# A two-block transformer forward pass on one core: projection work reordered around the decay masks, and the residual added inside the expert accumulators

## The chip, the cores and the metric

The kernel runs on one core of a Trainium2 chip. The metric is device time in microseconds (us), from start to end of one execution. Every weight and the input come from HBM, and the 256 x 1024 result goes back to it.

TensorE (PE) multiplies matrices into PSUM, eight banks of 128 x 512 fp32. VectorE (DVE) and ScalarE (ACT) move data out of PSUM and do elementwise work, GpSimd (POOL) does a little, and SyncE (SP) issues nearly all DMAs. Each engine runs its own program in order and waits on semaphores that the others raise.

## The reference, cut to what matters

There are 256 tokens of width 1024. The first block has a token mixer (a spatial gating branch and a gated delta rule branch) and a mixture of 32 experts. The second block has two attention layers, each with a gated feed-forward network.

```python
# first block
qkv = silu(causal_dwconv(dn_qkv, dn_conv_w))          # 4 taps along the tokens
q, k, v = split(qkv)                                  # 8 heads of 128 each
q = q * rsqrt(sum(q * q) + 1e-6); k = k * rsqrt(sum(k * k) + 1e-6)
G = cumsum(g)                                         # in chunks of 64 tokens
decay = exp(where(causal, G_i - G_j, -inf))
lmat = where(strict, beta * (k @ k.T) * decay, 0)     # solved as (I + lmat)^-1
attn = (q @ k.T) * decay
h = layer_norm(ALPHA * h + mix)                       # ALPHA = 2 ** 0.25
ffn = hier_moe(h)                                     # two of 32 experts a token
h = layer_norm(ALPHA * h + ffn)                       # the end of the first block
# second block
h = h + even_mixer(rmsnorm(h), ...)                   # begins with a projection of width 448
```

## The kernel before

**Weights.** The weights stream through a ring of SBUF slots, 2 MB each, filled by SP in the fixed order of `stream_items`. The mixer uses four slots and the experts six. SP refills a slot when its last reader has signalled.

**A projection tile.** Products are made of three fp32r matmuls each: high x high, high x low, low x high. So each half of a slot (a pair in the code) must be split first: ACT copies it rounded into a high part (`split_high`, `next_high`, L1067 to L1085), then DVE subtracts that from the slot and leaves the low part (`split_low`, L1565). `split_pairs` numbers the pairs. PE waits in `split_chunk` (L407) for the low part, then `project_split` issues 48 matmuls of 128 x 256 into one bank. There are two buffers for the high parts, so the high part of pair n waits until PE has finished pair n - 2.

**Order in the mixer.** The four tiles of `w_pa` (pairs 13 to 16) come before four key tiles (`dn_k`, 17 to 20), four query tiles (`dn_q`, 21 to 24) and four value tiles (`dn_v`, 25 to 28). After the second value pair of tiles come the column sums of the squared keys (`square_sums`, L570), then the last two value tiles, key-key products in `chunk_pairs`, the query sums, the first half of `dn_z`, the key transposes, the query-key products, and the second half of `dn_z`. All of these take their bank from a rotation of four (`take` without a bank); a fixed bank is given otherwise. A bank that is taken again waits until its reader has emptied it.

**Decays.** Four groups of matmuls (`Gb`) and two more (`Gc`) give sums of the log decays. DVE clips them, ACT takes the exponentials (L1151 to L1158), and DVE multiplies them by masks of 64 x 64 blocks (L1662 to L1674). DVE then clears the first four columns of six staging buffers (`stage_zero`, L1678).

**Convolution.** For each tile ACT copies two 128 x 256 halves out of PSUM into staging buffers, adding the bias (L1187), multiplies each by the last of the four taps (L1195), and splits the next pair (`next_high`, L1196). DVE splits the low part and adds the three other taps (L1700). ACT then applies SiLU two tiles late, squares the result, and for the keys and the queries `inverse_norm` turns the column sums into factors by Ln and Exp; DVE multiplies by them (`normed`, L1680).

**Experts and the seam.** The expert loop (`Fori` over 16 pairs of experts) adds each expert's output into four PSUM banks (`acc0` to `acc3`) by one-hot matmuls (`scatter`). The banks are opened by a product of the identity with a column of zeros (L722). After the loop DVE raises `experts_done` (L2006), ACT and DVE split the two pairs of the first weight of the second block (`lora`, pairs 45 and 46), and `residual` (L1807) computes h * ALPHA + acc for four pieces of 128 x 512, each followed by its statistics; `layer_norm` (L1528) subtracts the mean, waits for the factor and scales. The root-mean-square norm of the second block follows, then PE transposes and projects.

What sets the order everywhere is the program of each engine as written; no planner is at work.

## Time and profile before

| | |
|---|---|
| median of three runs | 1641.43 us (1639.04 to 1644.94) |
| the profiled execution's own time | 1639.78 us |
| its span, first to last instruction | 1638.0 us |
| PE busy with matmuls | 1433.2 us (87%) |
| DVE busy | 681.5 us (42%) |
| ACT busy | 542.7 us (33%) |
| DMA engines in the 20 slices of the experts | nearly always nine tenths or more |
| mean granted TensorE clock | 0.934 of full speed |

The busy shares are averages over stages with different limits. In the experts' stage the transfers are busy all the time; in the mixer and in the second block PE is busy nearly all the time, except for stretches in which it waits for ACT or DVE. "Idle before" in a row is the time in which the engine did nothing ahead of that row, with what ended it. In the rows that join several instructions, the first number is the start, the second the time from the first start to the last end.

### The profile page before, as it was taken

To read this page: it belongs to the slowest core of one execution; us is meant where nothing else is said; L and a number is where in the kernel's file an instruction comes from. 1 tells how busy PE (TensorE), PEld (TensorE's weight loads), DVE (VectorE), ACT (ScalarE), POOL (GpSimd) and SP (SyncE) were. 2 spreads that over 40 slices of the span, in tenths; PEclk is the share of its full clock that TensorE was granted. 3 is DMA by queue.
4 is the path that set the end of the run, shared out by engine and by line. 5 is a ranking of instruction groups with operands and counts; after the bars stand their busy time and mean duration, and the time that the engine had idled before them with its cause. 6 is when DMAs were issued, how large, how long until landed. Compare 5 with 4: busy or idle time off the path is not lost.

```text
span 1638.0 us, 25680 instructions
## 1 busy us (share of the span) xinstructions
PE 1433.2 (87%) x10764; PEld 1152.2 (70%) x10764; DVE 681.5 (42%) x1030; ACT 542.7 (33%) x861; POOL 46.8 (3%) x53
## 2 busy tenths in 40 slices
PE   6999887999968888888888849958999987889997
PEld 6989887987855444444444429547999986689997
DVE  4435676535640110101101144574555546555554
ACT  2451686135320110100101024344433345553343
POOL 0000000400020000000000000000000000000000
PEclk8988999989979999999999979978999998999999
DMA  6531442211266999999999982202544532154420
GB/s 285 192 118 52 154 155 80 77 53 59 83 280 274 427 427 429 429 429 427 429 429 429 428 372 102 105 1 92 204 177 183 218 112 94 52 193 181 178 102 26
DMA packets 27434, 349.54 MB, mean 213 GB/s; under 512 B 3041, under 2 KB 3297, under 8 KB 4578
## 3 DMA queue, kind: packets, MB, share of 16 engines
q1 hardware_dynamic: 27218, 347.46, 52.9%
q8 instruction: 54, 0.88, 0.2%
q10 hardware_dynamic: 144, 1.05, 0.2%
q14 instruction: 18, 0.15, 0.0%
HBM read 347.45 MB, written 1.05 MB: 213 GB/s over the span
## 4 chain that ended last, share of the span: by engine, by line
PE 68%; DMA 14%; DVE 9%; ACT 5%; issue 2%; SPq 1%; PEldq 0%; POOL 0%; DVEq 0%; POOLq 0%; ACTq 0%
PE psum L405 67%; DMA ring<-in_w 14%; ACT pages L1050 2%; DVE slot_lo L1573 2%; ACT mix_hi L1079 1%; PE psum L474 1%; DVE pages L2036 1%; DVE pages L2068 1%; DVE pages L2040 0%; DMA ab<-in_w_ab 0%; ACT pages L1305 0%; DVE pages L1538 0%; PE psum L758 0%; PEldq L815 0%; DVE pages L1700 0%
## 5 line engine op out<-in xcount | busy, mean ns | idle before, releaser
L405 PE MATMUL psum<-ring,pages 128*64 128x256 f32 (+1 forms) x2564 | 361.2, 439 | 66.5 <-DMA ring<-in_w 47.8
L405 PEld LDWEIGHTS psum<-ring,pages 128*64 128x64 f32 x2564 | 186.9, 143 | 225.9 <-issue 81.9
L405 PE MATMUL psum<-x_hi,gu_hi 128*128 128x256 f32 x704 | 201.3, 286 | 3.8 <-DVE x_lo L1560 3.8
L405 PE MATMUL psum<-x_lo,gu_hi 128*128 128x256 f32 x704 | 201.2, 286 | 0.0
L405 PE MATMUL psum<-x_hi,gu_lo 128*128 128x256 f32 x704 | 201.1, 286 | 0.0
L405 PE MATMUL psum<-h_hi,mix_hi 128*128 128x256 f32 x512 | 151.8, 296 | 17.2 <-DVE slot_lo L1573 8.9
L405 PE MATMUL psum<-pages 64*64 64x64 f32 (+10 forms) x1752 | 135.6, 267 | 21.5 <-ACT pages L1050 10.8
L1573 DVE TENSOR_TENSOR slot_lo<-ring,mix_hi 128x2048 fp32r<-128x2048 f32 x44 | 102.3, 2329 | 120.0 <-ACT mix_hi L1079 119.8
L405 PE MATMUL psum<-h_lo,mix_hi 128*128 128x256 f32 x512 | 149.7, 292 | 0.0
L405 PE MATMUL psum<-h_hi,slot_lo 128*128 128x256 f32 x512 | 149.5, 292 | 0.0
L405 PEld LDWEIGHTS psum<-pages 64*64 64x64 f32 (+4 forms) x1752 | 109.8, 156 | 45.5 <-issue 20.2
L405 PEld LDWEIGHTS psum<-x_hi,gu_hi 128*128 128x128 f32 x704 | 137.1, 195 | 6.1 <-DVE x_lo L1560 2.4
L405 PEld LDWEIGHTS psum<-x_lo,gu_hi 128*128 128x128 f32 x704 | 137.1, 195 | 1.6
L405 PEld LDWEIGHTS psum<-x_hi,gu_lo 128*128 128x128 f32 x704 | 137.0, 195 | 0.0
L1976 DVE TENSOR_TENSOR pages<-pages,psum 128x256 f32<-128x256 f32 x32 | 13.5, 421 | 268.2 <-ACT pages L1302 268.2
L405 PEld LDWEIGHTS psum<-h_hi,mix_hi 128*128 128x128 f32 x512 | 103.6, 202 | 19.6 <-DVE slot_lo L1573 13.8
L2084 DVE TENSOR_TENSOR gu_lo<-ring,gu_hi 128x2048 fp32r<-128x2048 f32 x44 | 100.8, 2292 | 27.2 <-ACT gu_hi L1384 27.2
L474 PE MATMUL psum<-consts,pages 128*128 128x128 f32 x262 | 46.0, 338 | 73.9 <-DVE pages L2132 31.2
L405 PEld LDWEIGHTS psum<-h_lo,mix_hi 128*128 128x128 f32 x512 | 103.6, 202 | 0.1
L405 PEld LDWEIGHTS psum<-h_hi,slot_lo 128*128 128x128 f32 x512 | 103.2, 202 | 0.0
L1302 ACT ACTIVATE pages<-psum 128x256 f32<-128x256 f32 x32 | 12.3, 385 | 274.2 <-PE psum L405 274.2
L1079 ACT ACTIVATE mix_hi<-ring 128x2048 fp32r<-128x2048 f32 x44 | 84.0, 1908 | 44.2 <-PE psum L405 44.2
(220 smaller groups left out, 2120.4 us busy)
## 6 DMA issues: line engine op xcount, KB each, us to landing
ring<-in_w SPq DMA_DIRECT2D x96, 2048.0 KB, 18.0
ring<-in_ffn SPq DMA_DIRECT2D x44, 1536.0 KB, 6.5
ring<-in_w_in SPq DMA_DIRECT2D x16, 2048.0 KB, 8.1
ring<-in_e_in SPq DMA_DIRECT2D x3, 2048.0 KB, 15.8
ring<-in_w_pa SPq DMA_DIRECT2D x2, 2048.0 KB, 8.0
ring<-in_w_pb SPq DMA_DIRECT2D x2, 2048.0 KB, 8.7
ring<-in_w_o SPq DMA_DIRECT2D x2, 2048.0 KB, 8.1
ring<-in_e_out SPq DMA_DIRECT2D x2, 2048.0 KB, 15.0
```

The lines of the kernel that those rows point to most:

```text
L405: return pe.matmul(o, lhsT, rhs, start=start, stop=stop, skip_group_check=True)
L474: last = pe.transpose(o[:, j * P:(j + 1) * P], s, ident)
L1050: st.do(act_e.activation(o, i, func, **kw), name)
L1079: act_e.activation(high[:, 0:size], slot(n)[:, c * size:(c + 1) * size], ACT.Copy).then_inc(S("w_high"), 1)
L1302: act_e.activation(silu[:, r, :], psum[:, r, 0:T], ACT.Silu).then_inc(S("silu_ready"), 1)
L1573: ve.tensor_tensor(slot_low[slot_no(n)][:, sl], slot(n)[:, sl], high[:, 0:size], ALU.subtract).then_inc(S("w_split"), 1)
L1976: ve.tensor_tensor(acts[:, r, :], silu[:, r, :], psum[:, r, T:2 * T], ALU.mult).then_inc(free[r], 1)
L2036: do(ve.scalar_tensor_tensor(e[:, h2, :], bias, slope(g), v[:, 0:SPAN], ALU.mult, ALU.add), f"{sec}s{g}")
L2068: do(ve.tensor_tensor(e[:, :, sl], e[:, :, sl], z[:, :, b].unsqueeze(2).broadcast_to([P, 2, size]), ALU.mult), f"{sec}_probs" if b else None)
L2084: ve.tensor_tensor(gu_part["lo"][j % 2], slot(item_no[(nm, 0)] + j)[:, 0:gu_size], gu_part["hi"][j % 2], ALU.subtract).then_inc(S("gu_spli ...
```

## The change

In the mixer: ACT computes the decay exponentials before it splits the `w_pa` and the first key pairs, not after them. The six staging buffers are cleared earlier, behind the splitting of the `w_pa` input. DVE's multiplications by the masks move to the first value tile. ACT splits the next pair ahead of the last tap instead of behind it. For the value tiles DVE, not ACT, multiplies by the last tap. The square sums get banks 4 to 7, and the key-key products take rotating banks. DVE multiplies the keys by their factors ahead of the split of that place, not behind it.

At the seam: the accumulator banks are opened by ALPHA times the identity, multiplied with the normed tokens, so that they hold h * ALPHA + ffn when the experts are done. DVE takes the statistics and the first step of the norm straight from PSUM. The last pair of experts is written out behind the loop on ACT and DVE, and the two `lora` pairs are split inside it, into buffers of their own (pages 5 and 7). SP issues the first three weights of the second block before it reads the largest expert's count, not after.

```diff
...
         split_pairs = []
-        page_high = {n: part(f"w_hi{n}", n * PAGE, PAGE) for n in (1, 2, 3, 4, 5)}
+        page_high = {n: part(f"w_hi{n}", n * PAGE, PAGE) for n in (1, 2, 3, 4, 5, 7)}
         page_part = {n: part(f"in{n}", n * PAGE, PAGE).rearrange("p (k t) -> p k t", t=T) for n in (1, 2, 3, 4, 6, 8, 9)}
...
                     name = f"{part}_ss{q4}"
-                    o = take(name)
+                    o = take(name, 4 + q4)
                     for half in range(2):
...
             for g in range(2):
-                chunk_pairs(f"kk{g}", 4 + g, lambda j, r: (units(3)[:, unit(g, j), r], units(3)[:, unit(g, j), r]))
+                chunk_pairs(f"kk{g}", None, lambda j, r: (units(3)[:, unit(g, j), r], units(3)[:, unit(g, j), r]))
             square_sums("q", 7)
...
                 o = take(f"acc{n}", 4 + n)
-                mm(o, ident, col("zero").broadcast_to([P, HALF]), True, False)
+                mm(o, alpha_ident, piece(tm(0), n), True, False)
             pe.wait_ge(*V("onehot_ready", NB))
...
             highs = (page_high[2], page_high[3])
-            project_tokens("lora", [("e_in", 0)], highs, parts, spread_done("att0"), LORA)
+            project_tokens("lora", [("e_in", 0)], (page_high[5], page_high[7]), parts, spread_done("att0"), LORA)
             project_split("qB", [("e_in", 1)], highs, parts)
...
             input_high(page_part[8], fm(5), lambda i: V("ya_ready", i + 1))
-            split_high(18)
 
...
             act(mix, mix, ACT.Exp, "decay_ready", scale=-1.0)
+            split_high(18)
 
...
 
-            stage = lambda n: page(5)[:, n % 6 * 260:n % 6 * 260 + 260]
             act_e.wait_ge(*V("stage_zero", 6))
...
                     act_e.sem_inc(free[place[name][0]], 1)
-                    for half in range(2):
+                    next_high()
+                    for half in range(2 if part != "dn_v" else 0):
                         k = 2 * n + half
                         act(fm(pg)[:, k, :], stage(8 * s + k)[:, 4:260], ACT.Copy, "tapped", scale=col("conv", 3 * 24 + first + k))
-                    next_high()
                     for b2 in (at - 3, at - 2):
...
                     act_e.activation(actT[:, r, :], psum[:, 2 + r, 0:T], ACT.Copy).then_inc(free[2 + r], 1)
+                if last and phases >= 3:
+                    split_high(MIXER_PAIRS + 2)
                 for r in range(2):
...
                     y_high(r, slot_table[:, 0, bass.ds(it * 2 + (EXPERTS + r), 1)]).then_inc(S("y_high"), 1)
+
+            with act_e.Fori(0, EXPERTS // 2 - 1) as it:
+                expert_pair(it)
+            expert_pair(EXPERTS // 2 - 1, True)
             tables_at[0] = None
...
                 act_e.dma_start(page(10), io["c_attn"]).then_inc(S("attn_tables"), 16)
-            if phases >= 3:
-                split_high(MIXER_PAIRS + 2)
             layer_rstd(2)
...
                     h, b = piece(tm(0), n), n % NB
-                    do(ve.scalar_tensor_tensor(h, h, mean_var[:, b, 0:1], piece(gains, n // NB * NB), ALU.subtract, ALU.mult))
+                    src = bank_of(f"{banks}{n}") if banks else h
+                    do(ve.scalar_tensor_tensor(h, src, mean_var[:, b, 0:1], piece(gains, n // NB * NB), ALU.subtract, ALU.mult),
+                       f"{banks}{n}" if banks else None)
                 ve.wait_ge(*V("norm_rstd", no + 1))
...
                     h, b = piece(tm(0), n), n % NB
-                    ve.wait_ge(st.sem, start + n + 1)
+                    if banks:
+                        ve.wait_ge(*evacuated(f"{banks}{n}"))
+                    else:
+                        ve.wait_ge(st.sem, start + n + 1)
                     do(ve.scalar_tensor_tensor(h, h, rstd[:, b:b + 1], piece(gains, n // NB * NB + 1), ALU.mult, ALU.add),
...
             input_low(0, page_part[9], fm(5), page_part[8])
+            ve.wait_ge(S("h_split"), 4)
+            for n in range(6):
+                do(ve.memset(stage(n)[:, 0:4], 0.0), "stage_zero")
 
...
 
+            cd = ab[:, 128:160]
+
+            def masked_decays():
+
+                ve.wait_ge(*V("decay_ready", 1))
+                do(ve.tensor_tensor(mix, mix, chunk_mask("minus_first", UNITS), ALU.mult))
+                do(ve.tensor_tensor(mix_t, mix_t, decay, ALU.mult))
+                do(ve.tensor_tensor(decay, decay, chunk_mask("incl_up", UNITS), ALU.mult))
+                settle()
+                for b in range(NB):
+                    m = mix.rearrange("p (h b) t -> p h b t", b=NB)[:, :, b, :]
+                    do(ve.tensor_tensor(m, m, bc(ab[:, 16 + b * HEADS:16 + (b + 1) * HEADS], 2, [P, HEADS, CHUNK]), ALU.mult))
+                for q4 in range(4):
+                    ve.wait_ge(*evacuated(f"Gb{q4}"))
+                do(ve.tensor_copy(cd, exp_rows.rearrange("p (x t) -> p x t", t=CHUNK)[:, :, CHUNK - 1]))
+                settle()
+
             for at in range(24):
                 s, k = at // 8, at % 8
-                if at % 2 == 0:
-                    split_low(19 + at // 2)
+                if at == 16:
+                    masked_decays()
                 if at == 20:
...
                     normed("k", 3, 8)
+                if at % 2 == 0:
+                    split_low(19 + at // 2)
                 dst = fm(CONVS[s][1])[:, k, :]
                 src = stage(at)
-                ve.wait_ge(*V("tapped", at + 1))
+                if s < 2:
+                    ve.wait_ge(*V("tapped", at + 1))
+                else:
+                    ve.wait_ge(*V("staged", at + 1))
+                    do(ve.tensor_scalar(dst, src[:, 4:260], col("conv", 3 * 24 + CONVS[s][2] + k), None, ALU.mult))
                 for j in range(3):
-                    if j:
+                    if j or s == 2:
                         settle()
...
                                 ALU.add), "router")
+            do(ve.tensor_scalar(alpha_ident, ident, ALPHA, None, ALU.mult))
             ge = r11[:, 80:96].rearrange("p (b g) -> p b g", b=NB)
...
                     spread_slots(r, slot_table[:, 0, bass.ds(it * 2 + r, 1)])
+                if last and phases >= 3:
+                    split_low(MIXER_PAIRS + 1)
                 for r in range(2):
...
                     y_low(r, slot_table[:, 0, bass.ds(it * 2 + (EXPERTS + r), 1)]).then_inc(free[2 + r], 1)
+                if last and phases >= 3:
+                    split_low(MIXER_PAIRS + 2)
+
+            with ve.Fori(0, EXPERTS // 2 - 1) as it:
+                expert_pair(it)
+            expert_pair(EXPERTS // 2 - 1, True)
             st.last = (free[3], base[3] + EXPERTS)
...
                         y_low(0, slot_table[:, c, bass.ds(e + EXPERTS, 1)]).then_inc(S("more_split"), 1)
-                ve.wait_ge(*V("more_split", EXPERTS * (MAX_PASSES - 1) + BUILT))
+                ve.wait_ge(*V("more_scattered", EXPERTS * (MAX_PASSES - 1)))
             do(ve.memset(ab[:, 0:1], 0.0), "experts_done")
-            if phases >= 3:
-                split_low(MIXER_PAIRS + 2)
-            residual(ALPHA, [f"acc{n}" for n in range(4)], layer_stats)
+            ve.wait_ge(*V("scattered", EXPERTS + 2))
+            for n in range(4):
+                layer_stats(n, bank_of(f"acc{n}"))
             ve.wait_ge(*V("ln2_landed", 16))
-            layer_norm("ln2", 2, tm(1))
+            layer_norm("ln2", 2, tm(1), "acc")
             if phases < 3:
...
                         sp.dma_start(slot(n + 2), src).then_inc(landed[slot_no(n + 2)], 16)
+                early = moe_first + 3 * EXPERTS
+                if phases >= 3:
+                    for n in range(early, early + MORE):
+                        load(n, *items[n])
                 sp.wait_ge(*V("starts_ready", 1))
...
                 with sp.If(most > CAP):
-                    for n in range(moe_first + 3 * EXPERTS - SLOTS, moe_first + 3 * EXPERTS):
+                    for n in range(early - SLOTS + MORE, early):
                         sp.wait_ge(*released[n])
...
```

ACT's program from the splitting of the `w_pa` input (L1092 here, L1097 in the changed kernel) to the first key tile. `mix_hi` rows are high parts, `ab` and `pages` rows at 128x32 and 128x1024 are exponentials. Before:

```order
L1092 ACTIVATE in_86<-pages 128x512 x4
L1079 ACTIVATE mix_hi<-ring 128x2048 x4
L1041 ACT_TABLE_LOAD
L1050 ACTIVATE pages<-psum 128x512 x4
L1050 ACTIVATE ab<-ab 128x32
L1050 ACTIVATE pages<-pages 128x1024 x2
L1050 ACTIVATE pages<-psum,consts 128x256 x2
L1050 ACTIVATE pages<-pages,consts 128x256 x2
L1079 ACTIVATE mix_hi<-ring 128x2048
```

The same place in the changed kernel:

```order
L1097 ACTIVATE in_87<-pages 128x512 x4
L1046 ACT_TABLE_LOAD
L1055 ACTIVATE pages<-psum 128x512 x4
L1055 ACTIVATE ab<-ab 128x32
L1055 ACTIVATE pages<-pages 128x1024 x2
L1084 ACTIVATE mix_hi<-ring 128x2048 x4
L1055 ACTIVATE pages<-psum,consts 128x256 x2
L1084 ACTIVATE mix_hi<-ring 128x2048
L1055 ACTIVATE pages<-pages,consts 128x256 x2
```

The seven exponentials and their table load now stand before four high parts, and the next high part stands before the taps.

DVE's program of the changed kernel at the seventh and eighth query and the first value tile. Before, the five rows at the masks stood ahead of the first key tile's split, and no TENSOR_SCALAR stood among the value tiles:

```order
L1587 TENSOR_TENSOR slot_lo_61<-ring,mix_hi 128x2048
L1722 SCALAR_TENSOR_TENSOR pages<-pages,consts 128x256 x6
L1691 TENSOR_TENSOR pages<-pages,masks 128x1024
L1692 TENSOR_TENSOR pages<-pages 128x1024
L1693 TENSOR_TENSOR pages<-pages,masks 128x1024
L1697 TENSOR_TENSOR pages<-pages,ab 128x8x64 x2
L1700 COPY ab<-pages 128x32
L1587 TENSOR_TENSOR slot_lo_62<-ring,mix_hi 128x2048
L1718 TENSOR_SCALAR pages<-pages,consts 128x256
L1722 SCALAR_TENSOR_TENSOR pages<-pages,consts 128x256 x3
```

The masks stand between the last tile of the queries and the split for the third value tile.

DVE's program of the changed kernel in the last pair of experts, written out behind the loop:

```order
L2000 TENSOR_TENSOR pages<-pages,psum 128x256 x2
L1988 TENSOR_SCALAR spots<-pages 128x256 x2
L1587 TENSOR_TENSOR slot_lo_61<-ring,w_hi_80 128x1792
L1992 SCALAR_TENSOR_TENSOR y_lo<-psum,pages,y_hi 128x512 x2
L1587 TENSOR_TENSOR slot_lo_61<-ring,w_hi_81 128x1792
```

Before, the two rows of 128x1792 stood behind `experts_done` and ahead of four pairs of SCALAR_TENSOR_TENSOR and BN_STATS; those pairs are now four BN_STATS that read PSUM.

## Rows read from the trace of the kernel before

**Rows 1.** Stretch, length, busy of PE PEld DVE ACT POOL, clock, DMA share, GB/s

```profile
183.00:188.00 5.00, 4.45 (x21) 4.45 (x22) 4.86 (x8) 3.73 (x4) 0.00 (x0) 0.50 0.03 7
```

**Rows 2.** Waits of PE from 130 to 360: us in total, times, longest

```profile
PE psum L405 <- ACT pages L1050: 9.7, 3, 4.8
PE psum L405 <- DVE slot_lo L1573: 8.2, 4, 7.2
```

**Rows 3.** Chain of waits, 130 to 310: start, us, what

```profile
172.30 1.23 DVE pages L1663
...
183.56 8.11 PE psum L405 x48
...
221.95 11.78 PE psum L405 x96
...
240.69 8.47 PE psum L405 x48
...
255.11 2.49 DVE pages L1685 x4
...
268.14 8.42 PE psum L405 x48
...
285.30 13.80 PE psum L405 x160
```

**Rows 4.** PE in order of time, 227 to 241: start, us, instructions

```profile
233.55 3.62 PE L405 MATMUL psum<-pages,consts 128*128 128x256 f32 x16
```

**Rows 5.** ACT in order of time, 120 to 300

```profile
177.51 0.84 ACT L1050 ACTIVATE pages<-psum,consts 128x256 f32<-128x256 f32 x2 [5.31 <-DVE pages L1678]
178.47 0.91 ACT L1050 ACTIVATE pages<-pages,consts 128x256 f32<-128x256 f32 x2
179.28 1.89 ACT L1079 ACTIVATE mix_hi<-ring 128x2048 fp32r<-128x2048 f32 x1
...
238.57 1.28 ACT L1041 ACT_TABLE_LOAD   x1
239.86 2.42 ACT L1050 ACTIVATE pages<-psum,consts 128x512 f32<-128x512 f32 x4
242.16 2.20 ACT L1050 ACTIVATE pages<-pages 128x512 f32<-128x512 f32 x4
```

**Rows 6.** DVE in order of time, 120 to 300

```profile
181.21 2.29 DVE L1573 TENSOR_TENSOR slot_lo<-ring,mix_hi 128x2048 fp32r<-128x2048 f32 x1 [3.79 <-ACT mix_hi L1079]
183.42 2.96 DVE L1700 SCALAR_TENSOR_TENSOR pages<-pages,consts 128x256 f32<-128x256 f32 x6
```

**Rows 7.** DVE in order of time at the seam, 930 to 990

```profile
961.84 0.06 DVE L2006 MEMSET ab<- 128x1 f32 x1 [1.20 <-issue]
964.16 3.96 DVE L1573 TENSOR_TENSOR slot_lo<-ring,w_hi 128x1792 fp32r<-128x1792 f32 x2 [2.26 <-ACT w_hi L1079]
968.14 0.69 DVE L1817 SCALAR_TENSOR_TENSOR pages<-pages,psum 128x512 f32<-128x512 f32 x1
...
973.60 0.28 DVE L1532 BATCH_NORM_AGGREGATE tiny<-tiny 128x2 f32<-128x12 f32 x2
...
976.71 2.73 DVE L1543 SCALAR_TENSOR_TENSOR pages<-pages,tiny 128x512 f32<-128x512 f32 x4
```

**Rows 8.** ACT in order of time at the seam, 930 to 990

```profile
954.74 0.38 ACT L1305 ACTIVATE pages<-psum 128x256 f32<-128x256 f32 x1 [4.11 <-PE psum L758]
...
959.05 0.69 ACT L1294 ACTIVATE y_hi<-psum,pages 128x512 fp32r<-128x512 f32 x1 [3.35 <-PE psum L405]
...
962.43 3.28 ACT L1079 ACTIVATE w_hi<-ring 128x1792 fp32r<-128x1792 f32 x2 [2.69 <-DVE ab L2006]
```

**Rows 9.** PE in order of time at the seam, 950 to 984

```profile
982.14 2.18 PE L474 MATMUL psum<-consts,pages 128*128 128x128 f32 x9 [20.24 <-DVE pages L2132]
```

**Rows 10.** SP's issues, 925 to 962, in order of time

```profile
932.72 0.35 SPq L2299 DMA_DIRECT2D ring<-in_e_lora  x1
```

**Rows 11.** DMA issues by line, 925 to 962: KB each, median us to landing

```profile
ring<-in_e_lora SPq DMA_DIRECT2D x1, 1792.0 KB, 20.3
```

48 lines of the change are left out of this document (18 added, 30 removed).

## The prediction, made before the changed kernel had run

> **What bounds the kernel now.** The slices of the page come first. In the slices of the experts the transfers are busy at nine tenths or more, so that stage moves as a whole with whatever comes ahead of it and cannot be shortened by this change. In the mixer and in the second block PE is busy nearly all the time, so there only its waits and its clock can be won. The waits of PE in the mixer come next: 8.2 us for low parts from DVE, of which one wait is 7.2 us, and 9.7 us for results of ACT in three waits, the longest 4.8 us [rows 2]. The chain of waits then shows what each wait is. The long one ends at 183.56, when the third key tile starts. Ahead of it stand DVE's mask products from 172.30, ACT's staging of the first key tile at 177.51, which had been idle 5.31 us for DVE, a high part at 179.28 and a low part at 181.21 [rows 3, 5, 6]. PE pays twice for such a wait. After it the granted clock is 0.50 of full speed, the 1.2 GHz level [rows 1], and the tile at 183.56 takes 8.11 us; two tiles at full clock take 233.55 - 221.95 = 11.60 us, 5.80 each [rows 3, 4]. So a tile after a wait costs 2.3 us more; those at 240.69 and 268.14 cost 2.7 and 2.6 more [rows 3].
>
> At the seam PE stands idle for 20.24 us until 982.14 [rows 9]. That is one serial chain on DVE and ACT: `experts_done` at 961.84, ACT's two high parts from 962.43, DVE's two low parts from 964.16, the residual with its statistics from 968.14 to 973.60, the first step of the norm, and the first finished tokens from 976.71 [rows 7, 8].
>
> **The mixer, step by step.** I count in the clock of the profiled execution. The exponentials wait for the clipped decays, and ACT's next task ahead of the change is a high part that waits for PE; ACT idles there, so the exponentials cost nothing at their new place. With the staging buffers cleared long before, ACT stages the first key tile as soon as PE has it, and the third key tile starts 7.2 us earlier, at 176.3, with no wait.
>
> Can PE then go on without waits? Behind a full tile ACT needs 0.96 us to stage it (177.51 to 178.47) and 1.9 us for the high part (179.28 to 181.21), now without the taps between them, and DVE 2.2 us for the low part (181.21 to 183.42) [rows 5, 6]. That is 5.1 us of the 5.80 of a tile, which leaves 0.7 us. DVE's own work for a tile is 2.2 + 2.9 = 5.1 us, also below 5.80. So the three smaller waits of 1.0 us in all [rows 2] go as well. Eight tiles from 176.3 end at 176.3 + 8 x 5.80 = 222.7, where the key sums start; before it was 233.55 [rows 4]. Gain here 10.8 us.
>
> The key sums take 3.6 us [rows 4] and end at 226.3. Before, the next tile then waited for a bank that ACT's Ln had to empty (one of the three ACT waits). With the sums in banks 4 to 7 it waits only for its low part. DVE ends the taps of the eighth tile at 211.1 (tile full) + 0.96 + 1.9 + 2.2 + 2.9 = 219.1. The masks now stand here: 172.30 to 177.4, 5.1 us [rows 3, 5], to 224.2, and the low part to 226.4. The eleventh tile starts at 226.5, against 240.69 [rows 3]: gain 14.2. So the masks are hidden just to the end; had they been 2 us longer, PE would lose those 2 us.
>
> A value tile costs DVE two more multiplications of 128 x 256. The trace has none of this form here. The nearest rows are DVE's taps, 2.96 us for six [rows 6], 0.49 each; nothing is the lower bound. I take 0.4 each, since they read one tensor, so 3.7 us of taps a tile (2.9 to 3.9). DVE ends the ninth tile's taps at 230.1, the low part at 232.3. The twelfth tile runs from 232.4 to 238.2. ACT turns 230.1 into the key factors: SiLU and square 0.9 (estimated from the tap pair, 0.91 for two, and the four Exp, 2.20), table load 1.28, four Ln 2.3, four Exp 2.2 [rows 5], 236.8. DVE's tenth tile ends at 236.0 and the key products of `normed`, 2.4 us [rows 3], end at 238.4. The key-key products start at 238.5; before, `normed` ended at 255.11 + 2.49 = 257.6. Gain 19.1.
>
> The query side: ACT stages and splits the eleventh tile (2.8), loads SiLU (1.3), does SiLU and square (1.3), 242.2, then stages and splits the twelfth, 245.0. DVE's low part waits for 239.6 and ends at 241.8, its taps at 245.5, and the last square comes at 246.4. The first `dn_z` tile starts behind the last query sum at about 247.3, against 268.14 [rows 3]: gain 20.8. From there ACT and DVE are late, not PE. DVE: low part 247.7, taps 251.4. ACT: SiLU 0.4, table 1.28, Ln 2.3, Exp 2.2, table 1.28, staging of `dn_z` 0.9 and high part 1.9, 261.6. DVE: low part 263.9, query `normed` 2.4, 266.3. The query-key products start at 266.4, against 285.30 [rows 3]: gain 18.9. PE is idle some 3 us ahead of the last query sum and again ahead of 266.4, so two spells at the low clock are likely. The first falls on `dn_z`, where PE has time to spare. The second falls on the 13.80 us of [rows 3] that ran undisturbed before; I take 2.4 us for it (the three prices above are 2.3, 2.7 and 2.6), or nothing if PE's transposes keep the clock up. **Mixer: 18.9 - 2.4 = 16.5 us** (14 to 20). Behind that, up to the experts, the order is unchanged, and the experts' transfers start as much earlier.
>
> **The seam.** In the last pair ACT's copy ends at 954.74 + 0.38 = 955.1. The two high parts, 3.28 us, now run there, to 958.4; the last `y_hi` has to wait for PE until 959.05 in any case, and the one ahead of it takes 0.7, so it is on time to 0.1 us [rows 8]. They need the weight `e_lora` landed: 932.72 + 20.3 = 953.0, 2.1 us before 955.1 [rows 10, 11]. DVE's first low part (1.98, half of 3.96) runs beside them. The second stands behind the last `y_lo` and ahead of `experts_done`, which therefore moves from 961.84 to 963.8. Behind `experts_done`, before: 961.84 to 973.60, 11.8 us. Now: four statistics at 0.69 us each, 2.7 us, at 966.5. The norm from there is the same in number and size, 3.1 us to the first tokens (973.60 to 976.71), 969.7 [rows 7]. **Seam: 976.7 - 969.7 = 7.0 us**. The bounds: statistics from PSUM at 0.5 to 1.0 us each give 6 to 8, and the low clock after the wait can end a tile earlier or later, 1 us each way.
>
> The trace shows DVE with operands from both memories at this size: the residual reads PSUM and takes 0.69 us, the last step of the norm reads SBUF and takes 2.73 / 4 = 0.68 [rows 7]. The Trainium skill, "VectorE: DVE Perf Modes", in the section on the TRN2 errata, gives VectorE 120 cycles of fixed cost from PSUM against 58 from SBUF, an estimate of 0.065 us more for each of the eight instructions that now read PSUM. By that rule the seam would give 6.5 us and the forecast would be 0.5 us later; by the rows it gives 7.0. The rows decide.
>
> The rest: ALPHA times the identity is one small DVE instruction in the router's chain, 0.2 us. Opening the banks is the same four matmuls with other data, nothing. The early clears (six of 0.1 us) stand beside PE's decay sums, nothing. The SP loads moved ahead of the count were issued at once before too, nothing.
>
> **Sum.** 16.5 + 7.0 - 0.2 = 23.3 us. The profiled execution took 1639.78 us (span 1638.0 and 1.8 around it), so 1616.5; it lies 1.65 us below the median of 1641.43, and the median of the changed kernel should be **1618 us**.
>
> **The rivals.** (a) Only the front of the mixer holds. If DVE or ACT run late among the value tiles (the cover of the masks is 0.1 us, and ACT's switches of tables stand in the new chain), PE gets the 10.8 us of the front and gives back what follows: 10.8 + 7.0 - 0.2 = 17.6, 1623.8. For it: four table loads lie on the new path. Against: the sums above were made with them, and the last wait has 0.7 us of slack a tile until then.
>
> The trace has a table load of 1.28 us, and the next instruction starts 0.01 us behind it [rows 5]. The Trainium skill, "ScalarE: Activation LUTs", section "What ACT_TABLE_LOAD costs", gives 2.66 us for every switch, a drain of 1.38 among them. By that rule the four loads would make the path 5.5 us longer and the time 1623.5. The row shows no drain, so its chance is 0.02.
>
> (b) The seam gives nothing: the high parts wait for `e_lora`, because more transfers are in flight with it, and the last `y_hi` is late by 7 us. 23.3 - 7.0 = 16.3, 1625.1. Against: it landed 2.1 us before it is needed.
>
> (c) The other side, slower: the same wait, but long. ACT stands at `e_lora` with `y_hi` behind it, and PE's scatter, `experts_done` and all of the second block behind that. Each microsecond that it lands after 955.1 costs one. It is slower than before from 955.1 + 23.3 = 978 on; at 990 the time is 1618 + 35 = 1653. For it: the queue is full there. Against: all transfers of that stretch are done soon after 962.
>
> (d) The change doesn't do what it says: a wait that I didn't see keeps the first key tile's staging where it was and the chain at the seam as long, 1641.
>
> (e) More than forecast: no spell at the low clock ahead of the query-key products and luck with the clock at the seam, 2.4 + 2 and a lower price of the taps, 1: 1612.
>
> **How the numbers follow.** Forecast, 1613 to 1624: 0.66. (a) 0.14, the rule on table switches 0.02, (b) 0.07, (e) reaching below 1613: 0.05, (d) 0.03, (c) 0.03. Within 0.3%, 4.9 us, is about what a measurement of this kernel can't tell from no change. So faster 0.66 + 0.14 + 0.02 + 0.07 + 0.05 = 0.94, same 0.03, slower 0.03. The range takes in (e), (a) and (b) with a little above them for the bounds: 1611 to 1628.
>
> **What would show it.** Right: PE's wait ahead of the third key tile gone and that tile at 5.8 us; key sums starting at about 223, `dn_z` at about 247, query-key products at about 266; at the seam `experts_done` some 2 us later against the last copy of ACT, and PE's idle time at 13 us, not 20.24. Wrong: a wait of PE for a low part behind the masks, a wait of ACT for the landing of `e_lora`, statistics from PSUM well above 0.69 us, or a part of the mixer gain given back between 300 and 490.

## The result, and the profile after

The changed kernel takes 1615.88 us (median of 4 runs, 1612.46 to 1618.32) against 1640.24 us of the kernel before in the same comparison (4 runs, 1638.95 to 1644.94). The ratio is 0.9845, 95% interval 0.9816 to 0.9873. The forecast was 1618, with a range of 1611 to 1628. The span of the profiled execution fell from 1638.0 to 1615.2 us, by 22.8.

Waits of PE in the same part of the mixer (131.2 to 344): us in total, times, longest. They are to be compared with [rows 2].

```profile
PE psum L410 <- ACT pages L1055: 4.7, 2, 3.3
PE psum L410 <- DVE pages L1684: 3.3, 1, 3.3
...
PE psum L410 <- DVE slot_lo L1587: 0.4, 1, 0.4
```

The 8.2 us for low parts have become 0.4, and the 9.7 us for ACT 4.7. The wait of 3.3 us for DVE's query product (L1684), ahead of the query-key products, has grown: it was 1.24 us before. The chain that ended last, from 165 on, is to be compared with [rows 3]:

```profile
164.99 47.05 PE psum L410 x392
...
220.20 1.13 DVE pages L1691
...
225.07 2.29 DVE slot_lo L1587
...
265.27 2.50 DVE pages L1684 x4
267.81 15.33 PE psum L410 x160
```

The first row is what the forecast said of the front of the mixer: PE multiplies 47 us on end (the row begins where the view does), straight through the place of the wait of 7.2 us. Behind it the chain runs over DVE: the masks (L1691 and on), low parts, taps. The last row is the one that took 13.80 us in [rows 3].

The places at which PE still waits, in order of time (start, us, instructions, idle time before them and what ended it):

```profile
247.61 2.07 PE L410 MATMUL psum<-pages,consts 128*128 128x256 f32 x4 [3.26 <-ACT pages L1055]
...
267.81 0.91 PE L410 MATMUL psum<-pages 128*64 128x64 f32 x12 [3.35 <-DVE pages L1684]
```

And the granted clock (the figure behind the busy times of the five engines) in the stretch of [rows 1], and behind these two waits:

```profile
183.00:188.00 5.00, 5.00 (x44) 5.00 (x44) 4.26 (x7) 4.44 (x8) 0.00 (x0) 1.00 0.24 102
```

```profile
247.30:250.70 3.40, 3.09 (x10) 2.73 (x11) 3.29 (x6) 0.31 (x2) 0.00 (x0) 0.51 0.00 0
267.80:271.20 3.40, 3.38 (x64) 3.39 (x64) 2.76 (x2) 0.00 (x0) 0.00 (x0) 0.50 0.11 48
```

The stretch that ran at the 1.2 GHz level before runs at full speed. In this execution two spells of 3.4 us at the 1.2 GHz level are left, where the forecast put them.

**How stretches are compared.** Two profiled executions don't line up. The first tile of `w_pa` starts at 141.51 before and at 142.66 after, though the change touches nothing that PE waits for ahead of it; in the twelve experiments below this start lies between 139.67 and 144.91. So from here on every time in the mixer is counted from the first `w_pa` tile, and every time at the seam from ACT's last copy. The value transposes are the end of the mixer's changed part:

| counted from the first `w_pa` tile | before | after | gain |
|---|---|---|---|
| third key tile starts | 42.05 | 34.65 | 7.40 |
| key sums start | 92.04 | 80.73 | 11.31 |
| eleventh tile starts | 99.18 | 84.76 | 14.42 |
| first `dn_z` tile starts | 126.63 | 106.46 | 20.17 |
| query-key products start | 143.79 | 125.15 | 18.64 |
| value transposes start | 157.42 | 140.32 | 17.10 |

Four traces below hold the changed mixer instruction by instruction: this one, `mixer_only`, `splits_back` and `ident_moved`. Up to the query-key products they agree within 0.02 us (125.14 to 125.16). Behind them they don't: the value transposes start at 140.32, 141.27, 141.22 and 141.32. The last three are alike, and the trace above is the odd one, by 1 us. So a difference at the query-key products counts from a few tenths on, one at the value transposes only above 1 us, and the mixer's gain is 16.1 to 17.1.

**The seam.** DVE in order of time, to be compared with [rows 7]:

```profile
942.40 2.02 DVE L1587 TENSOR_TENSOR slot_lo<-ring,w_hi 128x1792 fp32r<-128x1792 f32 x1 [6.51 <-ACT w_hi L1084]
944.57 1.44 DVE L1992 SCALAR_TENSOR_TENSOR y_lo<-psum,pages,y_hi 128x512 fp32r<-128x512 f32 x2
945.93 2.02 DVE L1587 TENSOR_TENSOR slot_lo<-ring,w_hi 128x1792 fp32r<-128x1792 f32 x1
947.87 0.69 DVE L1535 BATCH_NORM_STATS2 tiny<-psum 128x6 f32<-128x512 f32 x1
947.89 0.06 DVE L2038 MEMSET ab<- 128x1 f32 x1
948.48 1.87 DVE L1535 BATCH_NORM_STATS2 tiny<-psum 128x6 f32<-128x512 f32 x3
950.46 0.28 DVE L1541 BATCH_NORM_AGGREGATE tiny<-tiny 128x2 f32<-128x12 f32 x2
950.88 2.72 DVE L1548 SCALAR_TENSOR_TENSOR pages<-psum,tiny,pages 128x512 f32<-128x512 f32 x4
953.52 2.73 DVE L1557 SCALAR_TENSOR_TENSOR pages<-pages,tiny 128x512 f32<-128x512 f32 x4
```

ACT, to be compared with [rows 8]:

```profile
940.40 0.38 ACT L1310 ACTIVATE pages<-psum 128x256 f32<-128x256 f32 x1 [4.11 <-PE psum L763]
940.68 3.28 ACT L1084 ACTIVATE w_hi<-ring 128x1792 fp32r<-128x1792 f32 x2
943.86 1.36 ACT L1298 ACTIVATE y_hi<-psum,pages 128x512 fp32r<-128x512 f32 x2
```

PE's restart and the weight's landing, for [rows 9] and [rows 11]:

```profile
958.95 1.33 PE L479 MATMUL psum<-consts,pages 128*128 128x128 f32 x5 [11.47 <-DVE pages L2164]
```

```profile
ring<-in_e_lora SPq DMA_DIRECT2D x1, 1792.0 KB, 20.1
```

From ACT's last copy to the first tokens it was 976.71 - 954.74 = 21.97 us and is 953.52 - 940.40 = 13.12: the seam gives 8.85 us. The other ten traces with the whole new seam have 13.12 or 13.13 as well. PE's idle time fell from 20.24 to 11.47. The order of L1535 and the memset of L2038 shows a detail that the forecast missed: `experts_done` comes when the second low part has just ended, with no idle time ahead of it.

**The balance.** Gains: 17.10 + 8.85 = 25.95. Losses: 1.15 ahead of `w_pa` (phase, see above), 1.07 in the router (below), 0.54 over the experts and 0.39 behind the seam, 3.15 in all. 25.95 - 3.15 = 22.80, the difference of the spans. This is one pair of executions. The medians of the same comparison differ by 24.4 us.

### The profile page after: what moved, and what is told of

Same layout as the page of the kernel before. It is cut to its first block, busy times and chain, and to the rows that moved or that the text cites. A ratio compares the mean times of both kernels' runs of the same rounds, so it can differ in the third digit from the quotient of the medians.

```text
span 1615.2 us, 25662 instructions
## 1 busy us (share of the span) xinstructions
PE 1432.0 (89%) x10764; PEld 1149.9 (71%) x10764; DVE 682.2 (42%) x1035; ACT 540.5 (33%) x853; POOL 46.8 (3%) x53
## 3 DMA queue, kind: packets, MB, share of 16 engines
q10 hardware_dynamic: 144, 1.05, 0.2%
HBM read 347.45 MB, written 1.05 MB: 216 GB/s over the span
## 4 chain that ended last, share of the span: by engine, by line
PE 69%; DMA 15%; DVE 9%; ACT 4%; issue 2%; SPq 1%; POOL 0%; DVEq 0%; POOLq 0%; ACTq 0%
PE psum L410 67%; DMA ring<-in_w 14%; ACT pages L1055 2%; DVE slot_lo L1587 2%; PE psum L479 1%; DVE pages L2068 1%; DVE pages L1722 1%; ACT mix_hi L1084 1%; DVE pages L2100 1%; DVE pages L2072 0%; DMA ab<-in_w_ab 0%; DVE pages L1548 0%; PE psum L763 0%; ACT pages L1310 0%; DVE pages L2155 0%
## 5 line engine op out<-in xcount | busy, mean ns | idle before, releaser
L410 PE MATMUL psum<-pages 64*64 64x64 f32 (+10 forms) x1760 | 145.6, 275 | 20.4 <-ACT pages L1055 10.2
L410 PEld LDWEIGHTS psum<-pages 64*64 64x64 f32 (+4 forms) x1760 | 115.3, 161 | 48.4 <-issue 24.1
L479 PE MATMUL psum<-consts,pages 128*128 128x128 f32 x262 | 48.1, 348 | 65.1 <-DVE pages L2164 22.8
L1055 ACT ACTIVATE pages<-psum 128x512 f32<-128x512 f32 (+4 forms) x82 | 48.0, 600 | 153.2 <-PE psum L410 126.9
```

What stands on the lines that cost most here:

```text
L410: return pe.matmul(o, lhsT, rhs, start=start, stop=stop, skip_group_check=True)
L479: last = pe.transpose(o[:, j * P:(j + 1) * P], s, ident)
L1055: st.do(act_e.activation(o, i, func, **kw), name)
```

## The experiments

Twelve kernels, each executed 4 to 8 times beside the kernel before. A ratio is always to that. Single executions of one kernel spread over 3 to 12 us here, so a difference of 3 us between two kernels is read from the stretches of the trace, and the times only bear it out.

### The two parts of the change alone

`seam_only` has the mixer of the kernel before, instruction by instruction, and the changed seam. `mixer_only` is the reverse; its core:

```diff
-                mm(o, alpha_ident, piece(tm(0), n), True, False)
+                mm(o, ident, col("zero").broadcast_to([P, HALF]), True, False)
...
-                if last and phases >= 3:
-                    split_high(MIXER_PAIRS + 2)
...
-            for n in range(4):
-                layer_stats(n, bank_of(f"acc{n}"))
+            if phases >= 3:
+                split_low(MIXER_PAIRS + 2)
+            residual(ALPHA, [f"acc{n}" for n in range(4)], layer_stats)
```

> The kernel before with only the seam of the change (high and low parts in the last pair, ALPHA times the identity in the accumulators, statistics and norm from the banks, SP's loads moved). Every instruction of the mixer stands as it was. Theory of the forecast (the two parts act apart, seam 7.0 less 0.2): 1640.2 - 6.8 = 1633.4. Reading of the two traces: from ACT's last copy to the first tokens 21.97 us before and 13.12 after, 8.85, less 1.06 us that PE stands longer ahead of the rank product: 7.8, 1632.4. Rival (the seam's gain is luck with the clock behind the wait, which goes when the stretch moves in time): 5 to 6, 1634.5 to 1635.

> The changed kernel with the seam as before and without ALPHA times the identity. Theory of the forecast: 1640.2 - 16.5 = 1623.7. Reading of the two traces: the value transposes start 17.1 us earlier against the first tile of w_pa, 0.5 us of it is given back up to the experts: 1623.6. If the two parts act apart, this gain and that of the seam alone add up to the 24.8 us of the whole. Rival (they share something, such as a granted clock that falls elsewhere): the two gains differ from the whole by over 2 us.

Measured: `seam_only` 1632.23 us, ratio 0.9954 (0.9933 to 0.9974), which is 7.5 us by the ratio and 6.5 by the medians (1638.73 before). `mixer_only` 1618.46 us, ratio 0.9894 (0.9874 to 0.9915), 17.4 us by the ratio and 20.3 by the medians. Together the two give 24.9 us by the ratios, the whole change 25.4 (0.0155 x 1640), and 26.8 against 24.4 by the medians. The intervals are about 3.4 us wide to each side, so the times alone don't settle whether the parts add up to within 2 us. The traces do: in `seam_only` copy to tokens is 13.13 us and the mixer is 157.40 long, as before; in `mixer_only` the mixer has the changed kernel's times and copy to tokens is 21.58. So the two parts act apart, as the sum of the forecast supposed, and the seam's gain isn't luck with the clock.

### The front of the mixer: three edits that need each other

`exps_back` puts the exponentials behind the 18th high part again, `masks_back` the masks ahead of the first key pair's low part, `exps_masks_back` both.

```diff
 # exps_back, ACT
+            split_high(18)
             for q4 in range(4):
                 v = await_full(act_e, f"Gb{q4}")
...
-            split_high(18)
 # masks_back, DVE
-                if at == 16:
+                if at == 0:
                     masked_decays()
```

> The changed kernel with ACT's exponentials behind the 18th high part again, where they stood before; nothing else. In the changed trace ACT stages the first key tile at 171.81. With the exponentials (table 1.28, then 4.3 us) from 168.0 on it is free at 173.6, 1.8 us late, and the third key tile starts 1.8 us late, plus 2.3 us for the low clock behind the wait: +4.1, of which the wait of 0.41 us ahead of the eleventh tile hides some, 1619.5. Rival (the exponentials cost only through the mask products that wait for them, and these now stand later): no difference, 1615.9.

> The changed kernel with the mask products ahead of the first key tile's low part again (the staging buffers are still cleared early and the exponentials early). They would run from 170.9 to 176.0 on DVE, where the low part of the third key tile starts at 174.84 in the changed trace: 1.2 us late, so PE waits 1.1 us ahead of the third tile, plus 2.3 us for the low clock: +3.4 there. DVE has 5.1 us more among the value tiles, where PE waited 0.41 us: -0.4. So 1618.9. Rival (masks are the whole cause of the long wait of 7.2 us before): +7 or more, 1623. Rival (DVE's slack absorbs it): 1615.5.

> The changed kernel with both the exponentials behind the 18th high part and the mask products ahead of the first key tile's low part, as before; the staging buffers are still cleared early. Counted from the start of w_pa's first tile, the third key tile starts at 42.05 in the kernel before, 34.65 in the changed one, 35.93 with the exponentials alone moved back and 35.58 with the masks alone. Theory (the two add up in a chain: exponentials to 30.9, masks 5.1 to 36.0, low part 2.3 to 38.3): 38.3, and the clearing of the buffers, which let ACT stage only behind the masks, had cost the other 3.8 us. Rival (exponentials and masks are the whole of the wait): 42. Rival (they don't add up): 36 to 37. Time: the changed kernel's +0 to +2, since the masks at this place give back about 3.5 us at the query sums.

Measured: `exps_back` 1613.94 us, ratio 0.9855 (0.9832 to 0.9878). `masks_back` 1611.10, 0.9829 (0.9807 to 0.9850). `exps_masks_back` 1616.32, 0.9861 (0.9838 to 0.9884). From the first `w_pa` tile:

| | third key tile | wait ahead of it | key sums | `dn_z` | value transposes |
|---|---|---|---|---|---|
| before | 42.05 | 7.2 | 92.04 | 126.63 | 157.42 |
| after | 34.65 | none | 80.73 | 106.46 | 140.32 |
| `exps_back` | 35.93 | 1.14 | 82.11 | 107.39 | 141.66 |
| `masks_back` | 35.58 | 0.76 | 81.75 | 102.47 | 136.78 |
| `exps_masks_back` | 38.10 | 3.29 | 85.75 | 106.47 | 141.70 |

The third key tile comes near the place where the theory had it: 1.28 us later for 1.8 expected, 0.93 for 1.1 or 1.2, and 38.10 for 38.3 with both. Two expected times missed, 1619.5 for `exps_back` and 1618.9 for `masks_back`, since each held 2.3 us for a spell at the low clock that didn't come. The exponentials alone cost 1.3 us, the masks alone 0.9, both together 3.45. In the times this doesn't show: `exps_back` can't be told from the changed kernel. The last 3.95 us up to 42.05 are in `exps_masks_back` no longer there. In the trace before, DVE idles 3.79 us between the clearing of the staging buffers and that low part [rows 6], while ACT, which had waited for the clearing, stages the tile and makes the high part [rows 5]; here the low part follows the masks at once. That points at the late clearing, though no kernel put it back by itself (the order of ACT's work on a pair changed on that stretch too). So the wait of 7.2 us was one chain of three links. That each edit alone would have left most of it is likely from this, but not shown: no kernel made one edit alone.

The other half of the result was in none of the expectations: with the masks back at the front the mixer is *shorter* than in the changed kernel, by 3.54 us at the value transposes and by 3.27 at the query-key products (121.88 for 125.15). DVE in `masks_back`, at the third key tile:

```profile
173.18 1.23 DVE L1691 TENSOR_TENSOR pages<-pages,masks 128x1024 f32<-128x1024 f32 x1
...
178.14 2.29 DVE L1587 TENSOR_TENSOR slot_lo<-ring,mix_hi 128x2048 fp32r<-128x2048 f32 x1
```

5.1 us of masks make PE wait 0.76 us there. In the changed kernel the same 5.1 us stand ahead of the eleventh tile (220.20 in the chain above), on the path that ends last: the query sums wait 3.26 us for it. `masks_back` has no wait at the query sums at all. My expectation priced only the wait of 0.41 us ahead of the eleventh tile and named the wrong sign for the whole. The time agrees in sign (1611.10 for 1615.88), but the two intervals overlap.

### The banks of the square sums, and the taps

```diff
 # squares_back, PE
-                    o = take(name, 4 + q4)
+                    o = take(name)
...
-                chunk_pairs(f"kk{g}", None, ...
+                chunk_pairs(f"kk{g}", 4 + g, ...
 # taps_back, ACT and DVE
-                    for half in range(2 if part != "dn_v" else 0):
+                    for half in range(2):
...
-                    do(ve.tensor_scalar(dst, src[:, 4:260], col("conv", ...), None, ALU.mult))
```

> The changed kernel with the banks of the key and query square sums taken in turn again (and the key-key products in banks 4 and 5), where the eleventh tile needs a bank that ACT's Ln empties. In the changed trace the key sums end at 227.01, the first SiLU behind them starts at 229.22 and the first Ln at 233.30. Theory (the bank was one of the waits won): the eleventh tile starts at 233.9 or so, not 227.42, +6.5 there; PE's later waits of 3.26 and 3.35 us belong to ACT and DVE and take a part of it: the value transposes +4 to +6.5 against the first tile of w_pa, time of the changed kernel +4 to +6.5. Rival (the query chain on DVE is the end anyway, the bank costs nothing): 0 to +1.

> The changed kernel with the first tap of the value tiles on ACT again (0.89 us for two there) and not on DVE (0.76 us for two, pitch 0.38). Theory (DVE ends last at the query sums, since the mask products stand among its value tiles): DVE ends 4 x 0.76 = 3.0 us earlier over the four value tiles, ACT later by 3.6 but with idle time: the wait of 3.26 us ahead of the last query sum shrinks, the time goes down by 1 to 3. Theory of the forecast (ACT's chain with its table loads is the end there, the tap's move takes 0.9 a tile off it): +1 to +3.6.

Measured: `squares_back` 1625.67 us, ratio 0.9924 (0.9899 to 0.9949); value transposes at 147.65, 7.3 us later than in the changed kernel, query-key products 8.9 later. Expected were 4 to 6.5. The medians differ by 9.8 us. PE in its trace, the eleventh tile, and ACT's load of the Ln table and the Ln that it waited for:

```profile
234.18 0.55 PE L410 MATMUL psum<-h_hi,mix_hi 128*128 128x256 f32 x1 [7.12 <-ACT pages L1055]
```

```profile
232.05 1.28 ACT L1046 ACT_TABLE_LOAD   x1
233.34 2.42 ACT L1055 ACTIVATE pages<-psum,consts 128x512 f32<-128x512 f32 x4
```

PE starts when the first Ln has read its bank. So the bank theory holds, and these two lines of the change are worth more than any other edit that was taken back: 7.3 us.

`taps_back` 1615.48 us, ratio 0.9861 (0.9838 to 0.9883): its time can't be told from the changed kernel's. In the trace the query-key products start at 123.91, 1.24 us *earlier* than in the four traces with the changed mixer. So moving the tap to DVE costs 1.2 us in this change. The cost doesn't arise at the query sums, where my theory had it: the last of them starts 0.38 us *later* in `taps_back`, behind a wait of 3.61 us and not 3.26. It arises behind them. ACT's last SiLU of a value tile waits for DVE's taps and starts at 108.58 instead of 109.82, again 1.24 us, and the table load, the Ln of the query norm and the query-key products follow it. The multiplication itself costs 0.38 us (L1718 0.35, the next instruction 0.38 behind its start), against the 0.4 that the forecast took.

### The parts of the seam

```diff
 # splits_back
-                if last and phases >= 3:
-                    split_high(MIXER_PAIRS + 2)
...
             do(ve.memset(ab[:, 0:1], 0.0), "experts_done")
+            if phases >= 3:
+                split_low(MIXER_PAIRS + 2)
```

> The changed kernel with the first two high and low parts of the second block behind experts_done again; the residual stays in the accumulators. Theory: experts_done 0.4 us earlier against ACT's last copy (7.1), then 6.3 us for the parts ahead of the statistics as in the kernel before (961.84 to 968.14): first tokens 5.9 us later, 19.0 us behind the copy and not 13.12; time of the changed kernel +5.9. The other part of the seam, the residual in the accumulators, is then worth 21.97 - 19.0 = 3.0. Rival (the forecast's own terms: the last low part delays experts_done by 2.0): the parts are worth 4.2 only, +4.2.

Measured: 1617.07 us, ratio 0.9872 (0.9851 to 0.9893). DVE behind the last pair (ACT's copy is at 936.50):

```profile
943.31 0.06 DVE L2033 MEMSET ab<- 128x1 f32 x1 [1.20 <-issue]
945.62 3.96 DVE L1586 TENSOR_TENSOR slot_lo<-ring,w_hi 128x1792 fp32r<-128x1792 f32 x2 [2.25 <-ACT w_hi L1084]
949.50 2.48 DVE L1534 BATCH_NORM_STATS2 tiny<-psum 128x6 f32<-128x512 f32 x4
...
955.16 1.40 DVE L1556 SCALAR_TENSOR_TENSOR pages<-pages,tiny 128x512 f32<-128x512 f32 x2
```

First tokens 18.66 us behind the copy (19.0 expected), PE idle for 17.22. So the early splits are worth 18.66 - 13.12 = 5.5 us and the residual in the accumulators 21.97 - 18.66 = 3.3 (2.9 against `mixer_only`, where `experts_done` comes as early as here). The time differs from the changed kernel's by 1.2 us in the medians and 4.4 by the ratios, less than 5.5. In this trace PE did the router product mostly at full clock and reached the rank product 3.8 us earlier against the value transposes (169.92 and not 173.74), which hides most of it in a single execution. The idle time of 1.20 marked "issue" ahead of the memset is the count's load and the branch. With the low part queued ahead of it this time runs beside the low part, and that is what the forecast's +2.0 for `experts_done` left out.

### ALPHA times the identity, and a lock between DVE and GpSimd

PE's gap ahead of the rank product was 5.18 us before. After:

```profile
456.72 0.85 PE L410 MATMUL psum<-pages,consts 128*128 128x32 f32 x3 [6.24 <-DVE pages L1911]
```

DVE and GpSimd (POOL) in the trace after:

```profile
450.67 1.14 DVE L1856 TENSOR_SCALAR pages<-consts 128x128 f32<-128x128 f32 x1
```

```profile
449.93 1.81 POOL L2264 MEMSET pages<- 128x2048 f32 x1
```

```diff
 # ident_moved: from behind the router's bias to behind the picks
-            do(ve.tensor_scalar(alpha_ident, ident, ALPHA, None, ALU.mult))
...
             do(ve.tensor_tensor(pick, r11[:, 320:384], r11[:, 384:448], ALU.add), "picked")
+            do(ve.tensor_scalar(alpha_ident, ident, ALPHA, None, ALU.mult))
```

> The changed kernel with ALPHA times the identity on DVE just behind the picks, where DVE idles 2.74 us for the rank product; nothing else. In the changed trace it took 1.14 us at 450.67, and ended at 451.81, when a memset of POOL that had run from 449.93 ended at 451.74; PE's gap ahead of the rank product was 6.24 us against 5.18 before. Theory (DVE had to wait for POOL's memset): here, with POOL idle, it takes 0.2 to 0.3 us and PE's gap is 5.18 again, time -1.1. Rival (the instruction itself is that long): it takes 1.1 us in the idle stretch; the gap is 5.18 all the same. The time can't tell these two apart, the duration does.

Measured: 1615.87 us, ratio 0.9870 (0.9849 to 0.9892). DVE and POOL:

```profile
449.11 1.53 DVE L1887 TENSOR_SCALAR pages<-pages 128x32 f32<-128x32 f32 x2
...
453.16 0.22 DVE L1911 TENSOR_SCALAR pages<-consts 128x128 f32<-128x128 f32 x1
```

```profile
448.79 1.80 POOL L2264 MEMSET pages<- 128x2048 f32 x1
```

The instruction takes 0.22 us where POOL is idle: the theory of the wait holds. But PE's gap is 6.58 us, not 5.18. Against the value transposes the router product had ended 4.2 us sooner, 2.6 of it by a higher clock in the product itself (next rows), so POOL's memset now lies over another one-input instruction of the chain: the pair of L1887, which takes 0.38 us in the trace after (L1888 there), takes 1.53. `mixer_only` settles that this isn't a matter of where the identity stands: it has no such instruction at all, its router product ends as early, its gap is 6.61 us, and the same pair (L1886 there) lies over the memset:

```profile
448.89 1.53 DVE L1886 TENSOR_SCALAR pages<-pages 128x32 f32<-128x32 f32 x2
```

In `seam_only` PE comes to the end of the router product as in the trace before, the identity lies over the memset, and the gap is 6.23. So the instruction costs 1.05 us where the router product runs at the low clock. Where it ends sooner, the memset costs as much without it, and the instruction almost nothing more: `splits_back`, which has it at its place, shows 6.71 against the 6.61. The router product in `ident_moved` and in the changed kernel (granted clock 0.70 and 0.50):

```profile
439.00:446.72 7.72, 7.71 (x48) 7.60 (x48) 1.27 (x2) 4.46 (x8) 2.81 (x3) 0.70 1.00 427
```

```profile
440.13:450.49 10.36, 10.35 (x48) 10.21 (x48) 1.27 (x2) 4.46 (x8) 5.45 (x5) 0.50 1.01 432
```

### Three versions that go further

`early_two`: the masks ahead of the first low part of `w_pa`, where DVE idled 6.45 us; and ALPHA times the identity at its old place in a form with two inputs. `best`: the early masks, `ident_moved`, and POOL's memset behind the picks. `best_norm`: a fourth edit, the query norm ahead of the last SiLU.

```diff
+            settle()
+            masked_decays()
             for n in range(4):
                 split_low(15 + n)
                 v = await_full(ve, f"w_pa{n}")
...
 # early_two
+            do(ve.scalar_tensor_tensor(alpha_ident, ident, ALPHA, ident, ALU.mult, ALU.mult))
 # best, POOL
+                pool.wait_ge(*V("picked", 1))
                 st.do(pool.memset(page(2, 3)...
 # best_norm, ACT
+            inverse_norm("q", 7)
             for at in (22, 23):
                 silu_block(at)
-            inverse_norm("q", 7)
```

> The changed kernel with two edits in different stretches. First, the mask products stand ahead of w_pa's first low part, where DVE idled 6.45 us in the changed trace and the exponentials are just done: 5.1 us of masks fit. Theory: no wait at the third key tile (34.65 from w_pa's start, 35.58 with the masks behind w_pa), and the 3.27 us pitch of the key sums without a wait: value transposes at 136.0 against 140.32 in the changed kernel and 136.78 with the masks behind w_pa; time -4.3. Rival (the masks delay w_pa's low parts, PE waits there): a wait of 1 to 2 us at w_pa, value transposes at 138 or more. Second, ALPHA times the identity at its old place, written with two inputs from SBUF (identity times ALPHA times identity). Theory A (VectorE's one-input tensor_scalar needs the port that it shares with GpSimd, a memset of which runs there; the two-input form is blocked only by a GpSimd instruction that reads): 0.2 to 0.3 us there, the next one-input instruction over the memset may be blocked instead. Theory B (any VectorE instruction waits for the memset): it ends with the memset again, some 1.1 us.

> The changed kernel with three edits: the masks ahead of w_pa's first low part; ALPHA times the identity behind the picks; and GpSimd's memset of the sorted tokens' tail behind the picks too, so that no GpSimd memset runs beside DVE's routing chain. Theory: mixer -4.3 as in the kernel with the early masks; PE's gap ahead of the rank product 5.2 us and not 6.24 (or 5.4 and not 6.6 where PE does the router product at full clock): -1.1. Time 5.4 below the changed kernel, 1610.5. Rival (the memset is then late for the sorted tokens, or delays something in the next stretch): the -1.1 is gone.

> The same three edits and a fourth: ACT takes the Ln and Exp of the query norm ahead of the last two SiLU of the value tiles, for which it waited 3.09 and 1.41 us with the masks moved back; the number of table loads stays. Theory: ACT starts the Ln some 3.5 us earlier, as soon as the query sums are full, the query products of DVE and the query-key products of PE 3 to 3.5 us earlier, where PE had waits of 1.87 and 2.89 us: value transposes at 132.7 to 133.2 from w_pa's start, time 3 us below that with three edits, 1607.5. Rival (the key transposes' copies or the low part ahead of the query products become the end): -1 to -2 only.

Measured:

| | median, us | ratio | value transposes from `w_pa` | from there to the rank product |
|---|---|---|---|---|
| after | 1615.88 | 0.9845 (0.9816 to 0.9873) | 140.32 | 173.74 |
| `early_two` | 1609.62 | 0.9819 (0.9798 to 0.9840) | 136.01 | 173.11 |
| `best` | 1614.21 | 0.9840 (0.9818 to 0.9861) | 136.41 | 176.24 |
| `best_norm` | 1606.07 | 0.9792 (0.9770 to 0.9813) | 130.17 | 174.19 |

The early masks give 4.3 us in the mixer as expected, with no wait at `w_pa`: in `early_two` they run on DVE from 144.15, and `w_pa`'s first low part follows at once.

```profile
144.15 1.22 DVE L1678 TENSOR_TENSOR pages<-pages,masks 128x1024 f32<-128x1024 f32 x1 [1.10 <-ACT pages L1055]
...
149.11 2.29 DVE L1587 TENSOR_TENSOR slot_lo<-ring,mix_hi 128x2048 fp32r<-128x2048 f32 x1
```

The form with two inputs isn't blocked. It takes 0.28 us in the middle of POOL's memset, and PE's gap ahead of the rank product is 5.38 us:

```profile
444.61 0.28 DVE L1856 SCALAR_TENSOR_TENSOR pages<-consts 128x128 f32<-128x128 f32 x1
```

```profile
443.87 1.81 POOL L2264 MEMSET pages<- 128x2048 f32 x1
```

`best` has its gap of 5.18 us back, as expected, and yet isn't shown to be faster than the changed kernel: behind the value transposes it got another spell at the 1.2 GHz level and reached the rank product 2.5 us later. The stretch from 285 to 295 in `best` (in `early_two` the clock reads 1.00 there):

```profile
285.00:295.00 10.00, 7.87 (x220) 7.74 (x217) 4.84 (x7) 0.00 (x0) 9.92 (x6) 0.83 0.16 64
```

Its expected 5.4 us are therefore not shown by its time, only by its stretches. `best_norm` removes every wait of PE for DVE or ACT between `w_pa` and the query-key products but one of 1.49 us, and runs them at full clock; its chain shows 13.79 us for the 160 instructions that took 15.33 above:

```profile
257.73 13.79 PE psum L410 x160
```

ACT in it: the query's Ln starts at 243.11, and the two SiLU stand behind a table load that was there anyway.

```profile
241.82 1.28 ACT L1046 ACT_TABLE_LOAD   x1
243.11 2.43 ACT L1055 ACTIVATE pages<-psum,consts 128x512 f32<-128x512 f32 x4
...
248.00 1.28 ACT L1048 ACT_TABLE_LOAD   x1
249.29 0.73 ACT L1055 ACTIVATE pages<-pages 128x256 f32<-128x256 f32 x2
```

That is 6.2 us on `best` in the mixer, twice what I expected: PE's wait of 1.87 us among the key transposes went, the one ahead of the query-key products fell from 3.35 to 1.49, and with them went the slow spell behind. The interval of `best_norm` lies wholly below those of the changed kernel and of `best`: it beats both. That of `early_two` overlaps the changed kernel's, so its 4.3 us rest on the trace.

## Why the prediction was right, point by point

- **Front of the mixer.** Forecast: third key tile 7.2 us earlier and no wait, key sums 10.8 earlier. Measured 7.40 and 11.31. The links of the chain through exponentials and masks are shown by the three kernels that put them back; the link of staging is read from the trace before and was not tested by itself. Right.
- **Eleventh tile.** Forecast gain 14.2, measured 14.42, with a wait of 0.41 us where the forecast had 0.2. That the sums needed banks of their own is shown: without them the value transposes come 7.3 us later.
- **Query side.** Forecast gains 20.8 at `dn_z` and 18.9 at the query-key products, measured 20.17 and 18.64. In `mixer_only` and `splits_back` no low spell fell on `dn_z`, and its gain was 20.9. The second spell was priced at 2.4 us. In the trace after, the 13.80 us became 15.33, so 1.5, and the mixer gives 17.1 for 16.5. In the three other traces with the same mixer they became 16.28, 16.22 and 16.34, so 2.4 to 2.5, and the mixer gives 16.1 to 16.2. So the price was right, and that the first trace shows a smaller one is luck with the clock: 3.4 us at the 1.2 GHz level there, 6.7 or more in the others.
- **"The masks are hidden just to the end."** This sentence failed, though its numbers were in the sum. It looked at PE's next tile only. The chain of waits behind it ran over DVE, and there 5.1 us of masks were in the open: 3.3 to 3.5 us of the mixer in `masks_back`, 4.3 in `early_two`. The same holds for the tap, which I priced rightly (0.38 for 0.4) and took as relief for ACT; on balance it costs 1.2.
- **Seam.** Forecast 7.0, measured 8.85. The step that failed is "`experts_done` moves by +2.0": it moved by 7.49 - 7.10 = 0.4 us against ACT's last copy. The 1.20 us of load and branch ahead of it run beside the second low part, which wasn't in my count. That is 1.6 of the 1.85 us; the four statistics came in at 2.6 for 2.7. Statistics from PSUM take 0.62 us each, 2.48 / 4 in `splits_back`. The first step of the norm, now fed from PSUM, takes 2.72 us for four against 2.73 for the four of the last step from SBUF, so no price of PSUM shows. The Trainium skill's rule on it ("VectorE: DVE Perf Modes", the section on the TRN2 errata), by which I had estimated 0.065 us more an instruction, isn't borne out by these rows.
- **ALPHA times the identity.** Forecast -0.2, measured -1.1. The instruction is as short as I said (0.22), but it ran into GpSimd's memset. I hadn't looked at what GpSimd does at its place. The error of 0.9 took back half of what the seam had over. It belongs to this trace: with a router product that ends sooner the loss is as large without the instruction (`mixer_only`).
- **The rivals.** (a) fell: the gain of the front was not given back behind it. In the changed code's order too the next instruction follows a table load at once: load at 232.05 for 1.28, Ln at 233.34 (`squares_back`). The rule of the Trainium skill, "ScalarE: Activation LUTs", "What ACT_TABLE_LOAD costs", with a drain of 1.38 us a switch, therefore doesn't hold here. (b) and (c) fell: `e_lora` was issued at 918.86 and took 20.1, so it had landed 1.4 us before ACT's copy began at 940.40. No kernel tried what happens if it is late. One argument against (c) was misread: in the trace before, the transfers of that stretch don't end soon after 962. The DMA engines are nine tenths busy until about 977. (d) and (e) fell.

The sum came out at 23.3 against 22.8 in the profiled executions because the errors offset one another: +0.6 in the mixer (which is luck, -0.3 or -0.4 in the three traces like it), +1.85 at the seam, -0.9 in the router, -2.1 in stretches that the change doesn't touch. So that the sum is close to half a microsecond is luck too. That the mixer gives some 16.5 us and the seam at least its 7.0 is not.

## What to carry to other kernels

Work that is "hidden" beside one engine's next step is only free if it is also off the chain that ends last further on: follow its own engine to the next place at which somebody waits for it. Here 5 us of masks beside busy PE cost 3 to 4 us at the query sums and behind, and they were free in an idle stretch some thirty microseconds *ahead* of the place they had first been taken from. And test the edits of a change one by one: the banks of the square sums were worth 7.3 us, two of the moves (the masks and the tap) had the wrong sign by the traces, and the exponentials, taken back alone, cost 1.3 us of the 7.2 us wait that they had a part in.
